# Fewer idle products on TensorE at the start of the woven attention and recurrence

## The reference

```python
def token_mix(x, ...):
    p = rmsnorm(x, P['norm_mix']) @ P['w_in']
    y_rg = rglru_mixer(...)            # linear recurrence, 256 columns
    y_rw = rwkv7_mixer(...)            # 4 heads x 64, matrix state, delta rule, frame by frame
    q_lat, q_rope, ckv, kr = mla_project(...)
    s = (q_lat . ckv + q_rope . kr) * MLA_SCALE          # 8 heads, block-causal mask
    o = softmax(s) @ ckv                                 # prompt; the sample also sees 256 past rows
    y = concat([y_rg, y_rw, o @ w_uv]) @ P['w_out']
    return x + y, new_state
```

## Time and profile before

| | us |
|---|---|
| median of 3 runs | 1833.26 (1831.84 to 1834.72) |
| the profiled execution | 1831.97 |
| its span, first to last instruction | 1829.9 |
| PE busy in it | 1759.7 (96%) |
| DVE busy | 1132.5 (62%) |
| ACT busy | 869.2 (48%) |

### The profile page before, as it was taken

The page is one execution under the profiler, slowest core; times in us unless marked ns, Lnnn a source line. Parts: engine busy times, 40 slices in busy tenths (PEclk is TensorE's granted clock), DMA queues, the critical chain, the costliest instruction groups (busy, mean ns, idle before and its releaser), DMA issues.

```text
span 1829.9 us, 38018 instructions
## 1 busy us (share of the span) xinstructions
PE 1759.7 (96%) x16242; PEld 1640.5 (90%) x16242; DVE 1132.5 (62%) x1976; ACT 869.2 (48%) x1589; POOL 239.2 (13%) x210
## 2 busy tenths in 40 slices
PE   7989898999999999999999899999999999999997
PEld 7976777999799999999999677789987999999997
DVE  7786676544478666665367966666444776656653
ACT  5454556553356444444345455555434654444432
POOL 0010000300014222221100100011000332222201
PEclk9999999999999999999999999999999999999999
DMA  6100001461022322223231000133510222222221
GB/s 244 68 8 1 4 27 56 164 219 59 24 89 74 105 93 93 93 93 104 73 139 47 9 3 3 37 140 120 191 53 29 93 93 93 93 93 93 93 93 61
DMA packets 38758, 149.53 MB, mean 82 GB/s; under 512 B 4416, under 2 KB 4576, under 8 KB 36928
## 3 DMA queue, kind: packets, MB, share of 16 engines
q1 hardware_dynamic: 36288, 131.05, 21.0%
q0 software_dynamic: 2304, 16.06, 2.3%
HBM read 139.68 MB, written 7.41 MB: 80 GB/s over the span
## 4 chain that ended last, share of the span: by engine, by line
PE 81%; DVE 11%; ACT 5%; issue 2%; DMA 0%; DVEq 0%; ACTq 0%; SPq 0%
PE PS L829 59%; PE PS L1019 13%; PE PS L1047 5%; PE PS L1038 2%; DVE wL L1950 1%; DVE wL L1946 1%; ACT wH L1441 1%; DVE hbL L2419 1%; DVE stat L2313 1%; DVE xT L1976 1%; ACT hb L1441 1%; DVE hL L1964 1%; ACT aP L1441 1%; PE PS L1295 0%; ACT L1441 0%
## 5 line engine op out<-in xcount | busy, mean ns | idle before, releaser
L1441 ACT ACTIVATE wH<-ring 128x1024 fp32r<-128x1024 f32 (+1 forms) x294 | 261.4, 891 | 331.7 <-PE PS L829 268.2
L829 PE MATMUL PS<-hH,wH 128*128 128x272 f32 x1760 | 382.4, 299 | 13.2 <-DVE hL L1959 8.1
L829 PE MATMUL PS<-hH,wL 128*128 128x272 f32 x1760 | 366.3, 289 | 0.0
L829 PE MATMUL PS<-hL,wH 128*128 128x272 f32 x1760 | 365.3, 289 | 0.0
L1950 DVE TENSOR_TENSOR wL<-ring,wH 128x1024 fp32r<-128x1024 f32 x182 | 230.7, 1269 | 184.5 <-ACT wH L1441 183.6
L829 PEld LDWEIGHTS PS<-hH,wH 128*128 128x128 f32 x1760 | 278.4, 189 | 28.4 <-issue 12.6
L829 PEld LDWEIGHTS PS<-hH,wL 128*128 128x128 f32 x1760 | 277.9, 189 | 0.0
L829 PEld LDWEIGHTS PS<-hL,wH 128*128 128x128 f32 x1760 | 276.3, 189 | 0.0
L1019 PE MATMUL PS<-hbH,wH 128*128 128x272 f32 x784 | 227.1, 290 | 1.2 <-DVE hT L2475 0.9
L1019 PE MATMUL PS<-hbH,wL 128*128 128x272 f32 x784 | 227.0, 289 | 0.0
L1019 PE MATMUL PS<-hbL,wH 128*128 128x272 f32 x784 | 225.6, 288 | 0.0
(11 more groups left out here) (374 smaller groups left out, 3522.9 us busy)
## 6 DMA issues: line engine op xcount, KB each, us to landing
ring<-wall SPq DMA_DIRECT2D x238, 512.0 KB, 3.3
lw<-lw_in POOLq DMA_DIRECT2D x2, 1856.0 KB, 7.5
xT<-x_in SPq DMA_DIRECT2D x4, 544.0 KB, 6.0
y_out<-hT SPq DMA_DIRECT2D x8, 272.0 KB, 2.1
mem<-mem_in POOLq DMA_DIRECT2D x2, 1024.0 KB, 5.1
mks<-mks_in POOLq DMA_DIRECT2D x2, 1024.0 KB, 5.7
mvs<-mvs_in POOLq DMA_DIRECT2D x2, 1024.0 KB, 8.7
memk_out<-mkp POOLq DMA_DIRECT2D x2, 1024.0 KB, 6.2
```

The costliest lines, as they stand in the source:

```text
L829: return e.matmul(out, lhsT=a, rhs=b, start=start, stop=stop)
L1441: return e.activation(out, in_, f, **kw)
```

## The change

The idle products ahead of score(2), score(3) and score(4) of attention and ahead of score_m of group 4 are left out: 2 + 1 + 2 + 2 = 7 products a layer, 14 in the program. The three a layer ahead of tokens of group 4 stay. Nothing else moves.

```diff
-KEEP_BUSY = {2: 2, 3: 1, 4: 2}
 BESIDE_FACTORS = ("", "aaa", "a", "a", "")
...
                 def recurrence():
                     for kind, g, b in REC_STEPS:
-                        if (kind, g) == ("score_m", NG - 1):
-                            keep_busy(2)
                         if kind == "tokens":
                             if g == NG - 1:
                                 keep_busy(3)
...
                     for u, (h, b) in enumerate(UNITS):
-                        if u in KEEP_BUSY:
-                            keep_busy(KEEP_BUSY[u])
                         score(u)
```

## The result

The changed kernel takes 1839.18 us (median of 6 runs, 1838.13 to 1842.54) against 1833.13 us for the kernel before beside it (6 runs, 1831.84 to 1834.72): ratio 1.0037, 95% interval 1.0025 to 1.005. It is **slower by about 6 us**. The forecast was 1833.0 us with a range up to 1836.7; the measured time lies above it, on the side of the third case. All six executions of the changed kernel have a mean granted clock of 0.982 to 0.984; the profiled execution of the kernel before has 0.993.

What follows compares the result with a forecast made beforehand. TensorE (PE, busy 96%) was the engine to relieve, with DVE covering most removed time. Path and clock, 2 x (-1.0 + 0.85) = -0.3 us, gave a forecast median of 1833.0 us, range 1830.2 to 1836.7 us.

Steps and rivals of the forecast that it cites:

- the third case: Slower case, chance 0.20: clock stays low over the dense work after 152.7; 2 x (-1.0 + 2.8) = +3.6 us, 1836.9 us.
- The cost of what is removed: PE's time for the seven products: 14 passes at 0.42 us, 5.9 us a layer, 11.8 us in the program.
- How much is on the path: Layer 0 replayed without the products: 1.0 us of 5.9 us a layer leaves the path, 4.9 us becomes PE waiting.
- Step (a): Ahead of score(2), 4 passes: score(2) comes some 1.7 us earlier, but maximum(2) and DVE only 0.5 us.
- Step (b): Ahead of score_m, 4 passes: score_m starts 1.2 us earlier, its reader MG only 0.5 us; nothing gained beyond the 0.5 us.
- Step (c): Ahead of score(4), 4 passes: cross(4,1) could start 0.76 us earlier and score(5) 1.0 us earlier.
- the replay: Step-by-step timeline of layer 0 without the products: 1.0 us off the path a layer, 2.0 us in the program, clock untouched.
- case 4: Chance 0.05: PE's time is the path, as the chain of waits has it; -11.8 us, 1821.5 us.
- The clock: New PE waits bring a further clock fall in each layer, costing 0.85 us a layer; bounds 0 and 1.4, 2.8 for two stretches.
- Case 2: Chance 0.26: the clock holds or its low stretches meet only waits; -2.0 us, 1831.3 us.

## Why the prediction was wrong

**The cost of what is removed** was right: 28 passes gone.

**How much is on the path** was right. The rows of layer 1 of the kernel before, where the clock was up from tokens(4) at 1042.02 on, give the distances free of the low stretch of layer 0:

```profile
1046.25 0.56 DVE L2313 TENSOR_REDUCE stat<-PS 128x1 f32<-128x384 f32 x1 [0.42 <-PE PS L829]
...
1050.85 0.68 DVE L2175 TENSOR_TENSOR MG<-PS,cst 64x512 f32<-64x512 f32 x1
...
1054.93 0.67 PE L1047 MATMUL PS<-XX,LG 64*64 64x64 f32 x8
...
1056.42 0.30 PE L829 MATMUL PS<-akH,aqH 100*128 100x128 f32 x1 [0.23 <-ACT aP L1441]
```

Step (a): maximum(2) comes 4.23 us after tokens(4) before and 143.60 - 139.77 = 3.83 after, 0.40 us sooner (0.5 told). Step (b): MG 8.83 and 148.18 - 139.77 = 8.41, 0.42 sooner (0.5 told), and score_m's PE waits 1.37 us instead. Step (c): cross(4,1) 12.91 and 152.01 - 139.77 = 12.24, 0.67 sooner (0.76 told), at a clock that is low already. score(5): 14.40 before, 14.05 in the changed kernel at the low clock, and 13.27 in the kernel with the products in the waits, 1.13 sooner (1.0 told, which was for a clock that is up). That kernel gains 2.4 to 3.0 us in all, where the replay of both layers says 2.0. One sign did not come as told: PE was to idle about 1.6 us ahead of the merge that reads MG, and in the changed kernel it waits 0.16 us there, because score_m, score(3) and turn(2) already ran at the low clock. In the kernel with only unit 4's group, where the clock was still up while these three ran, it waits 1.61 us. The chain's promise of the whole time of the products, case 4, was rightly set aside.

**The clock** is the term that failed, by its size: 0.85 us a layer, with 2.8 us as its bound. The mechanism was named, and the first guess of the place (waits near 144 and 145, a fall behind them) came true. The whole part from tokens(4) to the key projection behind unit 8, in layers 0 and 1 of before and of the changed kernel, is what prices it:

```profile
139.00:167.29 28.29, 27.29 (x206) 18.16 (x206) 19.80 (x53) 12.93 (x37) 0.00 (x0) 0.88 0.00 1
1042.02:1068.98 26.96, 25.85 (x205) 16.98 (x205) 19.81 (x53) 12.81 (x37) 0.00 (x0) 0.94 0.00 1
```

```profile
139.77:170.28 30.51, 27.82 (x192) 20.59 (x192) 19.85 (x53) 13.06 (x37) 0.00 (x0) 0.61 0.00 1
1044.67:1075.18 30.51, 26.21 (x191) 19.69 (x192) 19.85 (x53) 13.06 (x37) 0.00 (x0) 0.66 0.00 1
```

With the clock up the part takes 26.02 us in before's order (the kernel without the group ahead of score_m) and 24.89 us with the products in the waits. I take 24.89 for the changed kernel with the clock up too, which is an estimate. Then the low clock costs the changed kernel 5.6 us a layer, and before pays 2.3 and 0.9 us for its own short stretches. The net cost of the clock is thus 4.0 us a layer where the step put 0.85. With the path's -1.13 that makes +2.9 us a layer, 5.8 in the program, and 6.05 were measured.

What failed within the step is the length. It priced a fall as one stretch of the length seen in the earlier trace rows, 1.4 us when full of work. The stretches lasted 24 and 20 us. The price of a low microsecond was not too small: from cross(4,1) to the projection the changed kernel loses 18.27 - 13.11 = 5.2 us to 16.8 us of low clock (164.92 - 151.81 = 13.11 us is the kernel without the group ahead of score_m, with the clock up). Before loses 0.7 us there to a stretch of 3.4 us. That stretch lay in the same dense work and ended by itself, and I took its length as a property of the clock. That a new fall might last longer had to widen the range; it did not.

**The cases.** Case 3 named the mechanism, a low clock over the dense work after 152.7, and its sign, a low clock held past 159 us, came; its two stretches (+3.6 us) were still too few. Case 2 (the clock holds) is contradicted by the profile. Its argument, that no wait as short as the new ones was known to bring a fall by itself, is weakened by the kernel without unit 4's products, whose clock fell behind waits of 0.48 and 0.91 us.

**The Trainium skill** (TensorE: Matmul & The Clock Gate, "HAM oscillation"), set beside the sum as a warning, was on the right side: waits let the clock fall and what follows starts at half speed. Its own example has waits for DMA of about 3 to 5 us; here the clock fell behind waits of 0.81 and 1.37 us. The same page of the Trainium skill (Part 1: The HAM clock gate, "What's actually happening") says that activity releases the throttle; the rows here put a limit to reading that as "as soon as PE is busy again", since PE shows 3.00 of 3.00 us busy in window after window at 0.50.

## What to carry to other kernels

Price idle products by what the clock does after them, not by their own time: here 5.9 us of them a layer lay mostly beside DVE's work and held the clock up for more than 20 us of dense work. Where PE waits in a chain of small dependent products, replay the schedule without the fillers, see where the waits come out, and put the fillers into those waits and not ahead of work that is ready: five a layer in the waits beat before's seven, by 0.13 and 0.15% in two comparisons. A low stretch seen once gives no length for the next; ask what work would end it.

## What the runs showed of the hardware

That the low clock holds on was not expected: 24 and 20 us in the changed kernel, 27 and 17 us without the groups of units 2 to 4, with PE busy for most of the time by its rows. A run of long products ended it (six passes of 512 columns in 4.60 us). Why the real work in between doesn't is open. Products on a quarter of the array can hold the clock up, but neither their effect on a low clock nor the gaps between the short dependent products, which the modelled ends of PE's rows may hide, were tried by themselves. In the changed kernel this 512-column key projection stood near the end of the stretch:

```profile
165.24 2.07 PE L828 MATMUL PS<-ckv,lw 128*128 128x512 f32 x2
```

In the kernel without the groups of units 2 to 4 it stood at 166.28 and the clock came back only after 178, so this one product is not a sure end. Nor does an end always need a run of idle products: the short stretch of before from 162.8 us ended without one. A fall is not certain either: without unit 4's group alone ten executions spread over 12.4 us, so a single time would have said "no change" or "+12 us".
